# Weights cast in pairs, scratch loads in single slots, and a first mixer that fills both rings in turn

## The reference

```
xn  = RMSNorm(x)
xa, ga, u, v, gates = split(xn @ W_in)             # 1024 each, gates 2 x 1024
o_a = (RG_LRU(causal_conv4(xa)) * gelu(ga)) @ W_br_a
o_b = (gelu(u) * (Ws_masked @ LayerNorm(gelu(v)) + b_s)) @ W_br_b    # 128-position chunks
mix = (sigmoid(g_a) * o_a + sigmoid(g_b) * o_b) @ W_out
x   = x + RMSNorm(mix)
x   = x + RMSNorm((silu(hn @ W_gate) * (hn @ W_up)) @ W_ffn_out),  hn = RMSNorm(x)   # inner width 2816
```

## Time and profile before

| | |
|---|---|
| median of 3 runs | 2222.84 us (2221.68 to 2596.24) |
| profiled execution | 2223.14 us, span of the slowest core 2221.6 us |
| spans of the 8 cores | 2213.2 to 2221.6 us, granted TensorE clock 0.972 to 0.976 |
| PE busy | 2074.0 us (93%) |
| DVE, ACT, POOL busy | 1122.9, 993.7, 536.7 us |
| DMA moved | 443.09 MB; HBM read 444.02 MB, written 53.54 MB |

### The profile page before, as it was taken

One profiled execution on the slowest core, in us unless ns is written; L12 is line 12 of the kernel. 1 busy time (PEld: TensorE's weight loads), 2 busy tenths in 40 slices (PEclk: granted clock), 3 DMA queues, 4 the chain that ended last, 5 costly groups with the idle time before them and its releaser, 6 DMA issues.

```text
span 2221.6 us, 37221 instructions; the slowest of 8 cores (2213.2 to 2221.6 us)
## 1 busy us (share of the span) xinstructions
PE 2074.0 (93%) x10647; PEld 956.8 (43%) x10647; DVE 1122.9 (51%) x1577; ACT 993.7 (45%) x1545; POOL 536.7 (24%) x883
## 2 busy tenths in 40 slices
PE   4877599999799999999999999999999999999897
PEld 1433244433344444444444444444444444444443
DVE  3761477314665157822675156832675246832442
ACT  5851476103682157611773147711774136711310
POOL 3443254222332123201420122201321112201100
PEclk9999799999899999999999999999999999999999
DMA  9879699999999687558855687558854577557456
GB/s 211 144 129 201 145 193 203 187 232 265 231 247 237 192 267 223 157 157 238 279 162 147 180 253 240 154 152 242 270 171 147 177 240 236 158 153 234 155 153 217
DMA packets 229493, 443.09 MB, mean 199 GB/s; under 512 B 26672, under 2 KB 26736, under 8 KB 229296
## 3 DMA queue, kind: packets, MB, share of 16 engines
q1 hardware_dynamic: 197968, 383.75, 56.7%
q0 software_dynamic: 31328, 56.96, 17.4%
HBM read 444.02 MB, written 53.54 MB: 224 GB/s over the span
## 4 chain that ended last, share of the span: by engine, by line
PE 81%; DMA 7%; issue 4%; ACT 3%; DVE 3%; POOL 1%; SPq 0%; ACTq 0%; DVEq 0%; POOLq 0%
PE ps L551 80%; DMA mring<-wt 2%; DMA fring<-wsc 1%; DVE XC L824 1%; PE ps L728 1%; ACT junk L557 1%; DMA wsc<-mring 1%; DMA mring<-wsc 1%; ACT L557 1%; DMA fring<-wt 1%; POOL stats L625 1%; DMA xres<-xp 0%; DVE xres L755 0%; POOL stats L622 0%; ACT xsb L557 0%
## 5 line engine op out<-in xcount | busy, mean ns | idle before, releaser
L551 PE MATMUL ps<-xnT,mring 128*128 128x512 bf16 x2560 | 610.1, 385 | 32.7 <-DMA mring<-wt 22.1
L551 PE MATMUL ps<-hnT,fring 128*128 128x512 bf16 x2816 | 631.7, 380 | 2.7 <-DVE hnT L731 2.7
L551 PEld LDWEIGHTS ps<-hnT,fring 128*128 128x128 bf16 x2816 | 275.9, 98 | 336.4 <-issue 8.0
L557 ACT ACTIVATE T<-ps 128x512 f32<-128x512 f32 x259 | 152.0, 596 | 590.3 <-PE ps L551 570.5
L551 PEld LDWEIGHTS ps<-xnT,mring 128*128 128x128 bf16 x2560 | 246.1, 99 | 318.5 <-issue 50.9
L551 PE MATMUL ps<-fring,ffT 128*128 128x512 bf16 x1408 | 341.0, 380 | 10.0 <-DMA fring<-wsc 5.2
L1046 DVE SCALAR_TENSOR_TENSOR T<-T,ps 128x512 f32<-128x512 f32 x130 | 89.2, 688 | 362.9 <-PE ps L551 357.6
L1196 DVE SCALAR_TENSOR_TENSOR sgt<-sgt,ps 128x512 f32<-128x512 f32 (+2 forms) x182 | 122.7, 674 | 260.8 <-ACT sgt L557 258.5
L557 ACT ACT_TABLE_LOAD x180 | 230.9, 1283 | 31.1 <-PE ps L551 22.8
L1063 POOL TENSOR_TENSOR VM<-T 128x512 bf16<-128x512 f32 x64 | 81.0, 1266 | 549.2 <-DVE T L1046 466.5
L551 PEld LDWEIGHTS ps<-fring,ffT 128*128 128x128 bf16 x1408 | 134.3, 98 | 172.6 <-issue 22.7
(11 more groups left out here) (122 smaller groups left out, 1903.6 us busy)
## 6 DMA issues: line engine op xcount, KB each, us to landing
fring<-wsc SPq DMA_DIRECT2D x594, 256.0 KB, 3.1
mring<-wsc SPq DMA_DIRECT2D x536, 256.0 KB, 3.9
fring<-wt POOLq DMA_DIRECT2D x110, 256.0 KB, 8.9
mring<-wt POOLq DMA_DIRECT2D x104, 256.0 KB, 9.4
wsc<-mring SPq DMA_DIRECT2D x72, 256.0 KB, 8.7
wsc<-fring SPq DMA_DIRECT2D x66, 256.0 KB, 8.4
xres<-xp SPq DMA_DIRECT2D x31, 512.0 KB, 8.2
yp<-xres SPq DMA_DIRECT2D x31, 512.0 KB, 6.5
```

The lines of the kernel that those rows point to most:

```text
L551: P.op("pe", lambda e: e.matmul(out, lhsT=lhsT, rhs=rhs, start=start, stop=stop), reads=reads, writes=writes, cost=max(27.0, n / 2.4 + 2.5))
L557: P.op("act", lambda e: e.activation(out=out, in_=in_, func=func, **kw), reads=reads, writes=writes, cost=165.0 + 0.833 * n + 93.0 * aps + ...
```

## The change

The 138 pieces are laid out as 69 pairs in `wt` (69 x 128 x 2048) and in `wsc`. `PAIRS` names them: neighbours of XA, GA, U, V, OUT and FO, FG with FU of the same index, and each gate piece with the branch piece that follows it in the order (GTA with BRA, GTB with BRB). A casting load and a store now carry a whole pair into or out of two neighbouring slots. Scratch loads stay piece by piece, each into one slot. `STORE_AT` goes by the pair's first piece, so GTA is now stored at its first fetch like its partner BRA: 206 pieces are cast instead of 214, in 103 DMAs, and 69 stores take the place of 138. `mring` has 10 slots instead of 9; the room comes from `wsS`, a small constant that moves into block 21 of the ffn's `ffT`. While `mixer(0)` is laid out, `mr.other = fr`: its pairs go to `mring` and `fring` in turn, so it has 18 slots, of which OUT holds four in each ring. The holding back of `fring` (`fr.after`) is gone.

```diff
-NM = 9
+NM = 10
+PAIRS = ([(b + c, b + c + 1) for b in (W_XA, W_GA, W_U, W_V) for c in range(0, 8, 2)]
+         + [(g + m, r + m) for g, r in ((W_GTA, W_BRA), (W_GTB, W_BRB)) for m in range(8)]
+         + [(W_OUT + c, W_OUT + c + 1) for c in range(0, 8, 2)]
+         + [(W_FG + j, W_FU + j) for j in range(22)]
+         + [(W_FO + j, W_FO + j + 1) for j in range(0, 22, 2)])
-    if pid < W_V or W_GTA <= pid < W_GTB or W_FG <= pid < W_FO:
+    pid = PAIRS[q][0]
+    if pid < W_V or W_FG <= pid < W_FO:
         return 1
...
-    wt = din("wt", [NPIECE, 128, 1024])
+    wt = din("wt", [NPAIR, 128, 2048])
...
+                def load_pair(self, q, store):
+                    if self.other is not None:
+                        self.turn += 1
+                        if self.turn % 2 == 0:
+                            return self.other.load_pair(q, store)
+                    self.i += self.i % 2
+                    s = self.i % self.n
+                    self.i += 2
+                    buf = self.buf
+                    cells = [(self.name, s), (self.name, s + 1)]
+                    two = buf[:, s:s + 2, :].rearrange("p a n -> p (a n)")
+                    P.op("pool", lambda e: e.dma_start(out=two, in_=wt[q, :, :]), writes=cells,
+                         dma_sem=self.pls[s], serial=True, cost=950.0, nbytes=1 << 20)
+                    if store:
+                        P.op("sp", lambda e: e.dma_start(out=wsc[q, :, :], in_=two), reads=cells,
+                             writes=[("wsc", q)], dma_sem=self.sts[s], serial=True, cost=70.0, nbytes=1 << 19)
+                    return buf, s, self.name
 
                 def get(self, pid):
-                    s = self.i % self.n
-                    self.i += 1
...
+                    q, h = PAIR_OF[pid]
+                    if h == 0:
+                        u = uses.get(q, 0)
+                        uses[q] = u + 1
+                        at = STORE_AT(q)
+                        self.open[q] = self.load_pair(q, u == at) if u <= at else None
+                    pair = self.open[q]
+                    if pair is not None:
+                        buf, s, name = pair
+                        s += h
                     else:
-                        P.op("sp", lambda e: e.dma_start(out=buf[:, s, :], in_=wsc[pid, :, :]), reads=[("wsc", pid)],
-                             writes=[cell], dma_sem=self.ls[s], serial=True, cost=70.0, nbytes=1 << 18)
...
+                        buf, s, name = self.buf, self.i % self.n, self.name
+                        self.i += 1
+                        P.op("sp", lambda e: e.dma_start(out=buf[:, s, :], in_=wsc[q, :, h * 1024:(h + 1) * 1024]), reads=[("wsc", q)],
+                             writes=[(name, s)], dma_sem=self.ls[s], serial=True, cost=70.0, nbytes=1 << 18)
...
-                fr.after = P.mark()
...
+            mr.other = fr
             run_stages(keyed(mixer(0), 0.0, 1.0))
+            mr.other = None
```

More of the change, by code:

```diff
@@ L39, with STORE_AT @@
 W_BRA, W_BRB, W_OUT, W_FG, W_FU, W_FO = 48, 56, 64, 72, 94, 116
-NPIECE = 138
-def STORE_AT(pid):
-    if pid < W_V or W_GTA <= pid < W_GTB or W_FG <= pid < W_FO:
+PAIRS = ([(b + c, b + c + 1) for b in (W_XA, W_GA, W_U, W_V) for c in range(0, 8, 2)]
[3 more added lines that the diff above has]
+         + [(W_FO + j, W_FO + j + 1) for j in range(0, 22, 2)])
+NPAIR = len(PAIRS)
+PAIR_OF = {pid: (q, h) for q, pair in enumerate(PAIRS) for h, pid in enumerate(pair)}
+def STORE_AT(q):
+    pid = PAIRS[q][0]
+    if pid < W_V or W_FG <= pid < W_FO:
         return 1
@@ L430, in build_program @@
     vs_o = dout("vs", [64, D])
-    wsc = nc.dram_tensor("wsc", [NPIECE, 128, 1024], BF16).ap()
+    wsc = nc.dram_tensor("wsc", [NPAIR, 128, 2048], BF16).ap()
     with contextlib.ExitStack() as es:
@@ L482, in build_program @@
         wsT = sb("wsT", [128, 8, 128], BF16)
-        wsS = sb("wsS", [64, 8, 64], BF16)
         RR = sb("RR", [128, 8, 128])
@@ L508, in build_program @@
         R_s_, K_R_s = ovf(20, 1, 256)
+        wsS_, K_wsS = ovb(21, 1, 512)
+        wsS = wsS_.rearrange("p (g t) -> p g t", g=8)[0:64]
         c64 = lambda a: a.rearrange("p (c t) -> p c t", c=NCH)
@@ L593, in __init__ @@
                     self.i = 0
-                    self.after = ()
-                def get(self, pid):
-                    s = self.i % self.n
-                    self.i += 1
[L599 to L606, removed]
-                    else:
-                        P.op("sp", lambda e: e.dma_start(out=buf[:, s, :], in_=wsc[pid, :, :]), reads=[("wsc", pid)],
-                             writes=[cell], dma_sem=self.ls[s], serial=True, cost=70.0, nbytes=1 << 18)
[L610 to L613, removed]
@@ new lines, in __init__ @@
+                    self.other = None
+                    self.turn = 0
+                    self.open = {}
+                def load_pair(self, q, store):
[15 more added lines that the diff above has]
+                    return buf, s, self.name
@@ new lines, in get @@
+                def get(self, pid):
+                    q, h = PAIR_OF[pid]
[8 more added lines that the diff above has]
+                        s += h
+                    else:
+                        buf, s, name = self.buf, self.i % self.n, self.name
+                        self.i += 1
+                        P.op("sp", lambda e: e.dma_start(out=buf[:, s, :], in_=wsc[q, :, h * 1024:(h + 1) * 1024]), reads=[("wsc", q)],
+                             writes=[(name, s)], dma_sem=self.ls[s], serial=True, cost=70.0, nbytes=1 << 18)
+                    return buf[:, s, :].rearrange("p (k n) -> p k n", k=NCH), buf[:, s, :], (name, s)
@@ L637, in create, with wcast @@
             cdma(lambda e: e.dma_start(out=cpk[:], in_=cpk_in), writes=[("cpk",)], nbytes=49152)
-            def wcast(i, dst, src, cn):
-                P.op("pool", lambda e: e.dma_start(out=dst[:], in_=src), writes=[(cn,)], dma_sem=w_sems[i], serial=True, cost=950.0,
+            def wcast(i, dst, src, cells):
+                P.op("pool", lambda e: e.dma_start(out=dst, in_=src), writes=cells, dma_sem=w_sems[i], serial=True, cost=950.0,
                      nbytes=1 << 19)
             def gate_constants():
-                wcast(0, wab, wa_in, "wab")
-                wcast(1, wxb, wx_in, "wxb")
+                wcast(0, wab[:], wa_in, [("wab",)])
+                wcast(1, wxb[:], wx_in, [("wxb",)])
                 dve(8, lambda e: e.tensor_scalar(out=ba2[:], in0=cpk[:, C_BA:C_BA + 8], scalar1=0.5, scalar2=None, op0=ALU.mult),
@@ L664, in row_loads @@
             def row_loads():
-                wcast(2, wsT, ws_in, "wsT")
-                wcast(3, wsS, wss_in, "wsS")
+                wcast(2, wsT[:], ws_in, [("wsT",)])
+                wcast(3, wsS, wss_in, K_wsS)
                 cdma(lambda e: e.dma_start(out=hst_s[:], in_=sh_in), writes=[("hst_s",)], after=P.mark())
@@ L1016, in s_sampU @@
                             mm(64, ps[:, b, g * 64:(g + 1) * 64], vh_s[0:64, g * 128:(g + 1) * 128], wsS[0:64, g, :], True, True,
-                               K_vh_s + [("wsS",)], [("ps", b)])
+                               K_vh_s + K_wsS, [("ps", b)])
                     gu, tm = 0, 2
@@ L1333, in make_in_maps @@
         wss[b * 32:(b + 1) * 32, :, b * 32:(b + 1) * 32] = wst[0:32, :, 0:32]
+    wt = np.stack([np.concatenate([wt[a], wt[b]], axis=1) for a, b in PAIRS])
     shared = dict(wt=f(wt), cpk_in=f(cpk), wa_bd=bd(g("w_a")), wx_bd=bd(g("w_x")), ws_t=f(wst), ws_s=wss,
```

## The result

The changed kernel takes 2201.44 us (median of 4 runs, 2197.27 to 2362.33) against 2222.43 us for the kernel before (median of 4, 2221.68 to 2596.24). The ratio is 0.99, 95% interval 0.9878 to 0.9923: a gain of 21 us, where 36 was forecast; the time lies between the forecast (2187) and the second rival (2207), inside the ranges that the prediction gives. The longest runs of both (2362.33 and 2596.24) were disturbed and do not enter the ratio. The profiled execution took 2202.11 us.

What follows compares the result with a forecast made beforehand. The prediction took the first mixer's gate stage to be short of DMA throughput and later stretches bound by matmuls; -28 - 5 - 3 - 2 + 2 = -36 us from 2223.14 us gave 2187, range 2162 to 2217 (forecast's own 2168 to 2210).

Steps and rivals of the forecast that it cites:

- second rival: First ffn: the gain is given back on full DMA, the stage ending 20 us later than forecast; 2207 us, chance 0.20.
- Gate stage and output weights, −28: 137.6 to 242.7 us: slots let DMA deliver casts earlier, cutting PE's waits and slow-clock matmuls; gain of 28 us.
- −5: From output to first ffn, 242.7 to 288 us: freer slots let next loads start beside OUT; gain of 5 us.
- +2 at the start: Start: 18 pieces queued at once beside the loads of x and b_s; a loss of 2 us.
- Price of a piece: Casting queue: 1.78 us per piece, going by bytes, so joining two transfers in one saves nothing.
- fourth rival: Gate stage: joined casts are faster in themselves, the chain's three casting loads shrinking by a third; 2172 us, chance 0.04.
- first rival: Before 137.6 us: idle time goes too, matmuls filling 16.5 us between 100 and 137.6; 2171 us, chance 0.18.
- First ffn and second mixer, −3: 288 to 557 us: 14.2 us of DMA leave, as much FG/FU casting comes, half fitting earlier; gain of 3 us.
- third rival: Start and 288 to 557 us: plain loads starve beside paired casts, costing 9 and 80 us; 2276 us, chance 0.08.
- Later tiles, −2: Later tiles: single pieces load as before, one more mring slot cuts 6.5 us of V waits; gain of 2 us.

Runs made afterwards that it cites:

- e2: The changed kernel without turn-taking: the first mixer fills mring alone (10 slots), no holding back of fring; 2244.18 us profiled, without an interval.
- e7: The kernel before with turn-taking of single casts in the first mixer, a tenth mring slot and GTA stored at first fetch; ratio 0.9801 to before.
- e1: The changed kernel with each pair cast by two DMAs with rows half as long, slots and order kept; ratio 0.9942 to before, 2200.41 us profiled.
- e10: The changed kernel with the ffn's FG, FU and FO alone cast and stored one by one; 2238.02 us profiled, no interval.
- e9: The changed kernel with the second mixer's XA, GA and U alone cast and stored one by one; ratio 0.9871 to before.
- e4: The kernel before with the tenth mring slot alone (wsS moved into ffT); ratio 0.9883 to before.
- e12: The changed kernel with the scratch laid out by piece, each piece's 256 KB together; ratio 0.9867 to before.

## Why the prediction held, and which terms were wrong

- **Gate stage and output weights, −28, with −5 behind it and +2 at the start: right in sum, in part by luck.** By the 1300th load the median core is 30 us ahead (31 forecast), and e2 shows that it is the turn-taking. The reason given for the 28, 18 slots, was right: the first output unit stands at 214.6 us in the median (215 forecast), DMA does 0.91 where it did 0.61, and the granted clock of the gate stage is 0.94 instead of 0.92. That it needed pairs was not claimed. (In that sum, 6.04 us at a clock of 0.59 would take 3.6 and not 4.5 us; the 28 does not depend on it.) But all 30 us are there by the 1200th load (229.7 instead of 259.6 us). The −5 behind the output units did not come, and the start, 1 us behind at the 32nd load, was 3 ahead at the 64th. e7, without pairs, is 30 us ahead at the 1200th load and 38 at the 1300th: in this gap the pairs give 8 back. Every core of the changed kernel waits 1.8 to 4.2 us for a casting load into `mring` between 235 and 560 us, and none of e7's does.
- **Price of a piece: right.** 1.68 us against 1.78; nothing like 2.0 us was saved for each DMA left out, and e1, which casts each pair by two DMAs, took 2200.41 us against 2202.11. The fourth rival is out, and the fixed part that the Trainium skill names ("DMA: Bandwidth & Descriptors", the anatomy of a DMA) does not show where transfers overlap.
- **Idle time before 137.6 us (first rival): some 4 of its 16 us went.** That is the lead at the 581st load. PE's 7.1 us of waits for casts there are gone, while its waits for ScalarE grew from 33 to 43 us (0 to 140 us, the slowest core of each).
- **First ffn and second mixer, −3: wrong.** Median +7 − 2 = +5 us, on the slowest core +11.3 − 2.4 = +9. I had looked for a new wait at `fring` alone, and had let the lead of four pairs cover it. What came is a wait as the third rival has it, at one place: five scratch loads of V issued from 266.6 us on, which land up to 26.7 us later beside paired casts for both rings. Between 240 and 310 us the eight scratch loads for `mring` land in 16.1 us (median), where twelve took 6.4 before. I priced this rival at 80 us, as if it held everywhere; it cost some 11 at most, and so the sign stayed. In time this comes near the second rival (20 us given back before 557 us), but its cause, moved FG and FU casts on a full DMA, is not borne out: the DMA share of the stretch fell from 1.01 to 0.89, waits for `fring<-wt` are 1.6 us, and e10, which casts them singly, keeps the 52 us. e9 shows that the pairs of XA, GA and U in the second mixer carry some 10 us. e1 shows that shorter packets alone give back only 2 of them, with PE waiting for the ffn's casts instead; how order and slots share the rest stays open.
- **Later tiles, −2: wrong twice, with opposite signs.** "They load single pieces as before" is where it failed. The tenth slot is worth 14 us there (e4), and I had bounded it by 6.5. The pair-wise scratch layout, which I had not costed at all, takes back much of it: the changed kernel gains 5 us there in the median, with the scratch by piece 12 (e12).
- **The slowest core counts.** The sum was made on one core, and the mean over the cores moved by 32 us, close to 36. That is luck in part, since the −5 and the −3 did not come and the later tiles gave more than 2. The spread of the cores went from 8 to 33 us: a core that escapes the waits for V ends near 2168 us (1 and 7), one that has both near 2200 (2 and 5). Which cores these are changes from run to run; why one escapes and its neighbour does not, I did not settle.

## What to carry to other kernels

Slots into which a queue can work ahead were worth more here than fewer, larger transfers: taking turns between two idle rings won 30 to 39 us up to the first ffn, a tenth slot 14 more behind, and joining transfers won nothing, because their price goes by bytes. A joined transfer also takes both its slots at once, asks for its second half before it is needed, and made the plain loads beside it land later; if it is stored joined, look at how later readers cut it. Where the slowest of several cores is the time, read the spread of the cores before the mean gain.

## What the runs showed of the hardware that was not expected

- Two busy DMA queues shared the engines packet for packet (861 to 860, 743 to 742), so the longer rows took the larger share: 71.2% to 33.2% and in the repeat 60.3% to 42.9% with casting rows of 4 KB, 76.5% to 26.9% with 8 KB. Eight plain loads then took 16.7 or 18.4 and 24.0 or 24.3 us to land (median) instead of 7.7 alone.
- Reading 2 KB out of every 4 KB made loads of 256 KB land in 3.3 to 3.5 us instead of 2.9 to 3.0, at nearly the same load of the plain queue between 900 and 2000 us (64.7% of the engines' time in the changed kernel, 66.3% in e12).
